# Splitting weight units by halves, moving the forget rows, and placing the output projection around the last state step of a two-model kernel

## The reference

```python
u = rmsnorm_2(h, attn_norm_w[l])
proj = u @ w_in[l]
gq, gk, gv, gz, gb, ga, fq, fk, fv, ff = jnp.split(proj, IN_SPLITS, axis=-1)
o_gdn = gated_deltanet_group(jnp.concatenate([gq, gk, gv], axis=-1), gz, gb, ga, ...)   # 4 heads of 128
o_fox = forgetting_attention_group(fq, fk, fv, ff, fgate_b[l])                          # 8 heads of 64
h = h + jnp.concatenate([o_gdn, o_fox], axis=-1) @ w_out[l]
h = h + swiglu(rmsnorm_2(h, ffn_norm_w[l]), w_gate[l], w_up[l], w_down[l])
```

## Time and profile before

| | us |
|---|---|
| median of 3 runs | 1022.68 |
| lowest, highest | 1018.86, 1023.31 |
| the profiled execution | 1022.64 |
| its span | 1020.8 |
| TensorE busy | 994.0 (97%) |
| VectorE, ScalarE, GpSimd busy | 620.7, 472.7, 113.1 |
| mean granted TensorE clock | 0.985 |

### The profile page before, as it was taken

One profiled execution on the slowest core, in us unless ns is written; L12 is line 12 of the kernel. 1 busy time (PEld: TensorE's weight loads), 2 busy tenths in 40 slices (PEclk: granted clock), 3 DMA queues, 4 the chain that ended last, 5 costly groups with the idle time before them and its releaser, 6 DMA issues.

```text
span 1020.8 us, 15770 instructions
## 1 busy us (share of the span) xinstructions
PE 994.0 (97%) x6364; PEld 866.0 (85%) x6364; DVE 620.7 (61%) x884; ACT 472.7 (46%) x818; POOL 113.1 (11%) x117
## 2 busy tenths in 40 slices
PE   8999999999999999999999999999999899999996
PEld 7988777879989999997778789877877799999885
DVE  4964456558865654756544669965642566666542
ACT  6334545457445533545533676634332454443432
POOL 1000122000400001012300023121200001111000
PEclk9999999999999999999999999989996999999999
DMA  8735444544556742330035435311110355555551
GB/s 293 289 125 206 138 151 165 182 172 146 206 203 216 280 165 83 125 129 38 1 127 203 165 129 178 131 60 42 42 42 1 117 193 173 199 178 194 170 202 42
DMA packets 23372, 150.55 MB, mean 147 GB/s; under 512 B 3548, under 2 KB 3832, under 8 KB 5896
## 3 DMA queue, kind: packets, MB, share of 16 engines
q1 hardware_dynamic: 22960, 149.39, 42.1%
q10 hardware_dynamic: 344, 0.18, 0.1%
HBM read 148.50 MB, written 1.05 MB: 147 GB/s over the span
## 4 chain that ended last, share of the span: by engine, by line
PE 88%; DVE 6%; ACT 1%; DMA 1%; issue 1%; SPq 1%; POOL 0%; ACTq 0%; POOLq 0%; DVEq 0%
PE psum L677 85%; DVE ring_parts L1874 2%; DMA ring<-in_weights 1%; DVE R L2158 1%; PE psum L756 1%; PE psum L1071 1%; ACT high_parts L1479 1%; PE psum L1368 0%; ACT R L1486 0%; DVE R L2221 0%; PE psum L1077 0%; PE psum L1239 0%; SPq L618 0%; POOL small L2415 0%; PE psum L1200 0%
## 5 line engine op out<-in xcount | busy, mean ns | idle before, releaser
L1874 DVE TENSOR_TENSOR ring_parts<-ring,high_parts 128x1024 fp32r<-128x1024 f32 (+1 forms) x272 | 332.8, 1264 | 166.5 <-ACT high_parts L1479 165.6
L1479 ACT CAST high_parts<-ring 128x1024 fp32r<-128x1024 f32 x268 | 267.3, 1048 | 213.7 <-PE psum L677 166.1
L677 PE MATMUL psum<-xT_parts,high_parts 128*128 128x256 f32 (+1 forms) x960 | 218.3, 286 | 1.5 <-DVE ring_parts L1874 1.0
L677 PE MATMUL psum<-xT_parts,ring_parts 128*128 128x256 f32 (+1 forms) x672 | 193.0, 287 | 0.0
L677 PE MATMUL psum<-high_parts,R_parts 128*128 128x512 f32 (+1 forms) x592 | 177.1, 374 | 4.0 <-DVE R_parts L2327 1.8
L677 PE MATMUL psum<-high_parts,xT_parts 128*128 128x512 f32 (+1 forms) x528 | 174.0, 406 | 2.0 <-DVE xT_parts L519 2.0
L677 PEld LDWEIGHTS psum<-xT_parts,high_parts 128*128 128x128 f32 x960 | 163.9, 190 | 3.0 <-DVE ring_parts L1874 1.7
L677 PE MATMUL psum<-R_parts,high_parts 128*128 128x256 f32 x832 | 160.6, 281 | 0.0
L677 PEld LDWEIGHTS psum<-R_parts,high_parts 128*128 128x128 f32 x832 | 131.6, 188 | 0.0
L677 PEld LDWEIGHTS psum<-xT_parts,ring_parts 128*128 128x128 f32 x672 | 127.5, 190 | 0.1
L677 PEld LDWEIGHTS psum<-high_parts,R_parts 128*128 128x128 f32 (+1 forms) x592 | 105.0, 179 | 24.6 <-issue 3.3
(11 more groups left out here) (297 smaller groups left out, 1093.0 us busy)
## 6 DMA issues: line engine op xcount, KB each, us to landing
ring<-in_weights SPq DMA_DIRECT2D x136, 1024.0 KB, 4.8
h<-in_x SPq DMA_DIRECT2D x4, 256.0 KB, 4.3
ring<-in_weights SPq DMA_DIRECT2D x4, 256.0 KB, 5.9
G<-in_gains SPq DMA_DIRECT2D x2, 512.0 KB, 7.6
out<-xn SPq DMA_DIRECT2D x2, 512.0 KB, 3.1
R<-in_ret_tabs SPq DMA_DIRECT2D x1, 768.0 KB, 11.7
tab<-in_tabs SPq DMA_DIRECT2D x1, 663.5 KB, 6.1
G<-in_p_t SPq DMA_DIRECT2D x1, 512.0 KB, 7.0
```

The costliest lines, as they stand in the source:

```text
L677: return pe.matmul(out, lhsT, rhs, start=first, stop=last, skip_group_check=True)
L1479: act.copy(as_r(hi), value).then_inc(sem("units_high"), 1)
L1874: return dve.tensor_tensor(as_r(value), value, value_of(hi), ALU.subtract)
```

## The change

- Splitting goes by halves: `up_to` counts halves and has an upper limit, and in the mixer stage each item is followed by at most one half. Elsewhere both halves still go together.
- `fin` 6 stands before `tok`, `fin` 7 between `A` 1 and `A` 2, the first value block before level 0; the other value blocks move up by one or two items each.
- `fox_rows` stands behind level 0 of the short chunk, and the two transfers behind `fv` 0 2.
- The rest of the normalisation chain is an item of its own (`Vg`); `Vg` 1 stands behind `Fo` 7, `Vg` 2 behind `Vo` 2.
- `mo` is four blocks of one row tile each; block 0 0 waits for the attention heads tile by tile instead of for the last head at its start. Their order is `mo` 0 0, `Vo` 2, `Vg` 2, `mo` 0 1, `mo` 1 0, `H`, `mo` 1 1. `H` is the turning of the delta rule's output, with its high and low parts on ScalarE and VectorE; those no longer force splits ahead of them (`behind`).
- The four banks of `w_down` are opened one by one, each before its first matmul.

```diff
-    u += tr_uses("mT0", 0, 2)
...
-    order = [("fin", 0), ("fin", 1), ("fin", 2), ("ss",), ("fin", 3), ("fin", 4), ("fin", 5), ("tok",), ("fin", 6), ("A", 1),
-             ("A", 2), ("fin", 7), ("A", 0)] + [("Lz", 0, c) for c in level_chunks(0)]
-    order += [("fv", 0, 0), ("Q", 1), ("fv", 0, 1), ("Qm", 1), ("Q", 2), ("fv", 0, 2), ("Qm", 2), ("kv", 1), ("fv", 1, 0),
-              ("kv", 2), ("fv", 1, 1), ("Fs", 0), ("fv", 1, 2), ("kv", 0)]
+    order = [("fin", 0), ("fin", 1), ("fin", 2), ("ss",), ("fin", 3), ("fin", 4), ("fin", 5), ("fin", 6), ("tok",), ("A", 1),
+             ("fin", 7), ("A", 2), ("A", 0), ("fv", 0, 0)] + [("Lz", 0, c) for c in level_chunks(0)]
+    order += [("fv", 0, 1), ("Q", 1), ("fv", 0, 2), ("Qm", 1), ("Q", 2), ("fv", 1, 0), ("Qm", 2), ("kv", 1), ("fv", 1, 1),
+              ("kv", 2), ("Fs", 0), ("fv", 1, 2), ("kv", 0)]
...
     order += [("W", 1), ("Fs", 7), ("W", 2), ("Fo", 5), ("Vn", 0), ("Fn", 7), ("Ft", 6), ("Vo", 0), ("gz", 1, 1), ("Vn", 1),
-              ("Fo", 6), ("Ft", 7), ("Vo", 1), ("Fo", 7), ("Vn", 2), ("mo", 0), ("Vo", 2), ("mo", 1)]
+              ("Fo", 6), ("Ft", 7), ("Vo", 1), ("Fo", 7), ("Vg", 1), ("Vn", 2), ("mo", 0, 0), ("Vo", 2), ("Vg", 2),
+              ("mo", 0, 1), ("mo", 1, 0), ("H",), ("mo", 1, 1)]
...
+        elif kind == "H":
+            u += tr_uses("mT0", 0, 2)
...
-            done = [1]
-
-            def up_to(u):
-                while done[0] <= min(u, NU - 1):
-                    if IS_SPLIT[done[0]]:
-                        split(done[0])
-                    done[0] += 1
+            halves = [2]
+
+            def up_to(u, at_most=2 * NU):
+                left = at_most
+                while left and halves[0] < 2 * min(u + 1, NU):
+                    if IS_SPLIT[halves[0] // 2]:
+                        split(halves[0] // 2, halves[0] % 2)
+                        left -= 1
+                    halves[0] += 1
...
-                aux.full(ins, (name, f), None if begun[0] else -HIGH)
+                aux.full(ins, (name, f), begun[0] - 1 - behind if behind else None if begun[0] else -HIGH)
...
-                    turn("mT0", f, lambda kt, t: R[:, R4 + 1024 + t * 512 + kt * P:R4 + 1024 + t * 512 + (kt + 1) * P])
+                    turn("mT0", f, lambda kt, t: R[:, R4 + 1024 + t * 512 + kt * P:R4 + 1024 + t * 512 + (kt + 1) * P],
+                         HIGH)
...
+            def mix_output(half, c, t):
+
+                if t == 0:
+                    unit["mo"] = next_unit(4)
+                w, product = unit["mo"]
+                bank = main.open(pe, ("mo", c, t)) if half else main.at(("mo", c, t))
+                if half == 0 and (c, t) == (1, 1):
+                    turn_ffn(0)
+                for k in range(4):
                     if half and (c, t) == (0, 0):
-                        wait_read(pe, aux, ("fo", FH - 1))
-                    if half == 0 and (c, t) == (1, 1):
-                        turn_ffn(0)
-                    for k in range(4):
-                        ins = parts3(product, bank, mix_src(4 * half + k, *rows[t]), w(k, slice(0, 512)),
-                                     half == 1 and k == 0, half == 0 and k == 3)
-                    if half == 0:
-                        main.full(ins, ("mo", c, t))
+                        wait_read(pe, aux, ("fo", 2 * k + 1))
+                    ins = parts3(product, bank, mix_src(4 * half + k, *rows[t]), w(k, slice(0, 512)),
+                                 half == 1 and k == 0, half == 0 and k == 3)
+                if half == 0:
+                    main.full(ins, ("mo", c, t))
...
+                elif kind == "H":
+                    pe.wait_ge(sem("mix_ready"), 2)
+                    turn_mix()
...
-            pe.wait_ge(sem("mix_ready"), 2)
-            turn_mix()
             for c in range(2):
-                mix_output(0, c)
+                for t in range(TT):
+                    mix_output(0, c, t)
...
-            banks = {(c, t): main.open(pe, ("dn", c, t)) for c in range(2) for t in range(TT)}
+            banks = {}
...
                     for t in range(TT):
+                        if k0 == 0:
+                            banks[c, t] = main.open(pe, ("dn", c, t))
...
+            def split_high(u, n):
+
+                if n == 0:
+                    act.wait_ge(sem(f"unit_in{u % RING}"), 16 * (u // RING + 1))
+                    if u >= HIGH:
+                        act.wait_ge(sem("units_used"), u - HIGH + 1)
+                hi, value = half_of(u, n)
+                act.copy(as_r(hi), value).then_inc(sem("units_high"), 1)
...
-                elif kind == "fv" and key == [0, 0]:
+                elif kind == "fv" and key == [0, 2]:
                     act.wait_ge(sem("fox_c"), 1)
                     for i in range(2):
                         act.dma_start(negc[(i + 1) * FH:(i + 2) * FH, :], negc_parts[:, i * TM:(i + 1) * TM]).then_inc(
                             sem("negc_in"), 16)
+                elif kind == "H":
+                    high_parts("mT0")
...
-                split_up_to(item + HIGH - 1)
-            high_parts("mT0")
+                split_up_to(item + HIGH - 1, 1)
...
-                    if c == 0:
-                        fox_rows()
...
+                    if c == 0:
+                        fox_rows()
...
-                    if c:
-
-                        dve.wait_ge(sem("go_square"), c)
...
-                split_up_to(item + HIGH - 1)
-            low_parts("mT0")
+                elif kind == "H":
+                    low_parts("mT0")
...
+                elif kind == "Vg":
+                    c = key[0]
+                    dve.wait_ge(sem("go_square"), c)
+                    s4 = slice(4 * c - 4, 4 * c)
...
+                    if c == 1:
+                        dve.wait_ge(sem("mix_gate"), 2)
+                    dve.tensor_tensor(R[:, m0:m0 + 512], on, R[:, R4 + (c - 1) * 512:R4 + c * 512],
+                                      ALU.mult).then_inc(sem("mix_ready"), 1)
+                split_up_to(item + HIGH - 1, 1)
```

More of the change, by code:

```diff
@@ L749, in project_b, with turn @@
                             main.full(ins, keys[n])
-            def turn(name, f, src):
+            def turn(name, f, src, behind=None):
                 bank = aux.open(pe, (name, f))
@@ L1273, in mix_src @@
                 return tuple(part[:, c0 - M:c0 - M + m] for part in fox_out(k - 4))
[L1275 to L1279, removed]
-                    if half and (c, t) == (0, 0):
-                        wait_read(pe, aux, ("fo", FH - 1))
-                    if half == 0 and (c, t) == (1, 1):
-                        turn_ffn(0)
-                    for k in range(4):
-                        ins = parts3(product, bank, mix_src(4 * half + k, *rows[t]), w(k, slice(0, 512)),
-                                     half == 1 and k == 0, half == 0 and k == 3)
-                    if half == 0:
-                        main.full(ins, ("mo", c, t))
+            unit = {}
+            def mix_output(half, c, t):
[6 more added lines that the diff above has]
+                for k in range(4):
+                    if half and (c, t) == (0, 0):
+                        wait_read(pe, aux, ("fo", 2 * k + 1))
[3 more added lines that the diff above has]
+                    main.full(ins, ("mo", c, t))
             unit = {}
@@ L1334, in _ @@
                     query_mask(*key)
-                elif kind == "Fn":
+                elif kind in ("Fn", "Vg"):
                     pass
+                elif kind == "H":
+                    pe.wait_ge(sem("mix_ready"), 2)
+                    turn_mix()
                 elif kind == "mo":
@@ L1470, in _ @@
             own = Marks(act, "act_step")
-            def split_high(u):
-                act.wait_ge(sem(f"unit_in{u % RING}"), 16 * (u // RING + 1))
-                if u >= HIGH:
-                    act.wait_ge(sem("units_used"), u - HIGH + 1)
-                for n in range(2):
-                    hi, value = half_of(u, n)
-                    act.copy(as_r(hi), value).then_inc(sem("units_high"), 1)
+            def split_high(u, n):
[5 more added lines that the diff above has]
+                act.copy(as_r(hi), value).then_inc(sem("units_high"), 1)
             wait, after_read, split_up_to = split_units(act, split_high, HIGH - 1)
@@ L1874, in low_part, with split_low @@
                 return dve.tensor_tensor(as_r(value), value, value_of(hi), ALU.subtract)
-            def split_low(u):
-                for n in range(2):
-                    dve.wait_ge(sem("units_high"), 2 * SPLITS[u] + n - 1)
-                    low_part(*half_of(u, n)).then_inc(sem("units_low"), 1)
+            def split_low(u, n):
+                dve.wait_ge(sem("units_high"), 2 * SPLITS[u] + n - 1)
+                low_part(*half_of(u, n)).then_inc(sem("units_low"), 1)
             wait, after_read, split_up_to = split_units(dve, split_low, HIGH - 1)
```

19 lines of the change are left out of this document (7 added, 12 removed).

## The result

| | before | after |
|---|---|---|
| median of the runs, us | 1023.31 (5 runs) | 1014.98 (5 runs) |
| lowest, highest | 1018.86, 1027.24 | 1014.67, 1017.61 |
| the profiled execution: span | 1020.8 | 1013.2 |
| mean granted clock in it | 0.985 | 0.987 |
| TensorE busy | 994.0 | 991.6 |

A forecast was written before the change was run, and what follows sets the result against it. TensorE's list bounds the kernel (busy 994.0 of 1020.8 us). From 1022.64 us, idle time - 4.95 (five waits gone, two new of 1.7) and clock - 3.4, together - 8.35, give 1014.3 us; range 1008.5 to 1019.8, 8 times in 10.

The forecast's parts named there:

- columns: TensorE's wait for the last decay row at `tok`: goes, as `fin` 6 stands in between; gain 1.39 us.
- The level 0 and `w_down` terms: Bank wait behind level 0 goes, gain 1.98 us; wait at the start of `w_down` goes with late opening, gain 1.09.
- The wait at the first scores: New wait at `Fs` 0 for the bank that `kv` 1 left: about 1.7 us, bounds 0 and 2.5.
- The wait at `H`: New wait where TensorE needs the chain of chunk 2, with two halves between the chains: 1.7 us, 0 to 2.5.
- Head 7: Wait before head 7's scores for head 4's low part: 2.86 us stays, gain 0, bound 11.4 with its low stretch.
- the first low stretch: Half clock at about 679 to 686 us, behind the level 0 wait: goes with it, worth 0 to 3.4 us, 3.4 taken.
- rival B: Clock falls behind the new wait at `Fs` 0 instead, so the first stretch only moves: 1017.7 us; chance 0.25.
- the long stretch: Half clock at about 767 to 783 us, behind the wait before head 7's scores: 8.55 us stays, gain 0.
- C's quick hand-overs: The two new waits, at `Fs` 0 and `H`, hardly appear: 1010.9 us; chance 0.08.
- F's late halves: Halves come late; TensorE waits 1.18 us at each of seven units from `fv` on, 8.3 us: 1022.6; chance 0.10.
- E's long loss of the clock: Clock falls at `Fs` 0 and stays low through the levels, 30 us costing 15: 1029 us; chance 0.04.
- D: Wait before head 7's scores is met at another moment, second low stretch shortens or goes: down to 1005.8 us; chance 0.07.

The follow-up runs named there:

- the second profile: The changed kernel run once more with no edit, for a second profile: 1017.74 us, span 1016.0.
- the third experiment: The changed kernel with no half of a weight unit split after the items from `gz` 1 0 to `Vo` 0: 1006.68 us, ratio 0.9833.

## Why the prediction was right, point by point

- **Which waits go.** All five as forecast: columns, `Q` 1, start of `mo`, delta output, `w_down`, together 8.35 us. Two reasons were finer than I had them. The columns' wait would have gone by the halves alone. For `mo` I named both the low part's place and the tile by tile waits; the place is enough. The level 0 and `w_down` terms were tested by themselves and hold; that the block `mo` 1 1 is what covers the 2.04 us of the delta output was not.
- **The wait at the first scores.** Forecast 1.7 (0 to 2.5), measured 1.34. TensorE arrived 4.8 us after the end of `fv` 1 0 (forecast 4.7), the key product that it waits for ended 6.0 us after it (forecast 6.35), because the second half began at 3.5 and not 3.75 and each of VectorE's instructions starts some 0.08 us before the one ahead of it ends. The recorded sum has a slip besides: its own terms give 6.29 and not 6.35 for VectorE, 4.8 and not 4.7 for TensorE, and so a wait of 1.5 us and not 1.7.
- **The wait at `H`.** Forecast 1.7, measured 1.72; the chain ended 7.2 us after `Vo` 2 (forecast 7.3).
- **Head 7.** Forecast: 2.86 us stays, as both halves still stand ahead of the low part. It is 2.86, and holding the halves back takes it away.
- **The clock.** This is the weak term, and that the total fits is in part luck. I gave 3.4 us to the first low stretch. It did go from 680 us, but rival B came true in part: 1.7 us were lost behind the new wait at the first scores. A low stretch elsewhere was one of my own signs of being wrong, and here it is. In the first profile the long stretch was shorter by 1.7 us, which I had put at 0, and this made up for it. In the second profile, with 12.0 us lost, the clock gave nothing at all, and the time was 1017.74, at rival B's 1017.7. Over the runs the truth lies between: the median 8.3 us below that of before, of which 5.3 are idle time. Against B I had set that the waits of 1.85 and 2.04 us brought no low clock. Two other kernels with the same two waits had it there, so that was true of an execution and not of the place. The 2.04 us were also no bank wait, as my sentence on B takes them: TensorE waited there for `xT_parts`, the data of its next matmul.
- **Rivals.** C's quick hand-overs, F's late halves (no wait of TensorE for a half in the stage) and E's long loss of the clock did not occur. D, the long stretch shorter or gone: it was shorter by 1.7 us in one profile and as long as before in the other; gone it was not in this kernel, but is what the third experiment made: its 8.55 us and the wait are what was left lying.

## What to carry to other kernels

When a profile of a busy engine shows a low clock right behind a wait among small matmuls, remove the wait first: here moving two pieces of VectorE work that no one needed yet away from in front of the awaited one was worth 9 us, though the wait itself was 2.6. When work is handed out in smaller pieces, look at each place where the rule still puts a piece in front of something that TensorE is about to need; a list of such places did more than the finer pieces. And the idle times within a stage can be taken from a single profile, as here, but its clock can't: a second profile of the same kernel told which low stretches were constant.

## What the runs showed of the hardware

- The granted clock can fall without any idle time of TensorE near it that the profile shows. In four of the ten profiles of kernels with the changed order it went to half from about 662 to 666 us (window at 660: 0.72 to 0.77), right behind the turnings of `tok` and eight more matmuls of 4 rows; in the other six, one of which has `tok` a little earlier, it stayed at 1.00 with the same matmuls. The Trainium skill, "TensorE: Matmul & The Clock Gate", section "Part 1: The HAM clock gate", says that the clock follows how busy the engine has been. The rows at 660 us, where the profile has TensorE busy for 5.00 of 5.00 us, neither bear this out nor refute it: the profile's busy share counts such small matmuls in full.
- Waits of 1.85 and 2.04 us between dense blocks left the clock at 1.00 in both profiles of the kernel before. In the kernel with only the forget rows moved windows there fell to 0.72 and 0.73, and in the kernel before with the halves held back to 0.78 and 0.68. The wait of 1.09 us at the start of `w_down`, also in front of dense matmuls, brought no low clock in any of its five profiles.
- Waits in front of small matmuls were followed by a low stretch each time: the 1.34 us behind the second `kv`, in front of scores of 64 rows, in seven of seven profiles (about 1.7 us lost by the windows), the 1.98 us before `Q` 1 in three of three (3.4 us), head 7's 2.86 us in eleven of eleven (6.85 to 8.55 us). In the profiles without the wait the stretch behind it was missing too. These three are also waits for a bank of PSUM; whether that or the small matmuls make the difference to the second point is not shown, though the 1.09 us were a bank wait as well.
- A stretch at half clock can cost less than half its length: the one behind head 7's wait cost 6.0 us where its windows gave 6.85.
